# Four products of a state-space scan summed by TensorE instead of being added on VectorE

## What is computed

```python
def s5_mixer(u, lam_re, lam_im, b_re, b_im, c_re, c_im, d, log_dt, w_glu, b_glu):
    ...
    bu = lax.complex(jnp.einsum('blgi,gpi->blgp', uf, jnp.real(b_bar)),
                     jnp.einsum('blgi,gpi->blgp', uf, jnp.imag(b_bar)))
    a = jnp.broadcast_to(lam_bar, bu.shape)
    _, states = lax.associative_scan(diag_combine, (a, bu), axis=1)
    y = (jnp.einsum('blgp,gip->blgi', jnp.real(states), c_re.astype(f32))
         - jnp.einsum('blgp,gip->blgi', jnp.imag(states), c_im.astype(f32))
         + d.astype(f32) * uf)
    y = jax.nn.gelu(y.reshape(B, L, S5_CH))
    y = y * jax.nn.sigmoid(y @ w_glu.astype(f32) + b_glu.astype(f32))
```

## Time and profile before

| | |
|---|---|
| median of three runs | 1843.37 us (1842.34 to 1846.21) |
| the profiled execution | 1846.9 us, its span 1845.1 us |
| TensorE busy | 1667.8 us, 90% of the span |
| VectorE busy | 838.0 us, 45% |
| state-space stretch, layer 0 | 113.2 to 193.9 us |
| state-space stretch, layer 1 | 703.0 to 783.2 us |

### The profile page before, as it was taken

How to read it: one execution, slowest core, us unless ns; L and a number is a source line. 1 busy time by engine, 2 the same in 40 slices (tenths; PEclk the granted TensorE clock), 3 DMA queues, 4 the chain that set the end, 5 groups by cost and what they waited for, 6 DMA issues and landing times.

```text
span 1845.1 us, 23055 instructions
## 1 busy us (share of the span) xinstructions
PE 1667.8 (90%) x9735; PEld 1468.3 (80%) x9735; DVE 838.0 (45%) x1339; ACT 494.1 (27%) x746; POOL 487.9 (26%) x198
## 2 busy tenths in 40 slices
PE   6989889879999898898888999889999988879996
PEld 5877577669999687666667999878888767679996
DVE  3979333324333498923422333338921232154543
ACT  1110330313443111051122444310002221144442
POOL 0000000018887000000003888500000000159883
PEclk9999879899999899987899999999999999889998
DMA  5544223145665453322324666465544312436662
GB/s 131 145 114 110 76 69 103 57 137 162 185 185 168 101 149 103 99 91 64 92 77 130 188 184 187 134 182 143 155 148 133 96 46 64 131 92 184 190 186 70
DMA packets 352775, 233.36 MB, mean 126 GB/s; under 512 B 20070, under 2 KB 339969, under 8 KB 352672
## 3 DMA queue, kind: packets, MB, share of 16 engines
q1 hardware_dynamic: 352672, 231.89, 43.2%
HBM read 230.77 MB, written 1.09 MB: 126 GB/s over the span
## 4 chain that ended last, share of the span: by engine, by line
PE 77%; DVE 13%; ACT 4%; DMA 2%; SPq 2%; issue 1%; POOL 1%; DVEq 0%; ACTq 0%; POOLq 0%
PE ps L1746 20%; PE ps L873 15%; PE ps L1729 6%; PE ps L1731 6%; PE ps L1730 6%; DVE WK L1383 6%; PE ps L856 3%; PE ps L858 3%; PE ps L857 3%; PE ps L895 2%; DVE WK L1541 2%; PE ps L1771 1%; DMA raw<-in_w_in_dram 1%; PE ps L910 1%; PE ps L1798 1%
## 5 line engine op out<-in xcount | busy, mean ns | idle before, releaser
L1111 POOL TENSOR_TENSOR w_lo<-raw,w_hi 128x1024 fp32r<-128x1024 f32 x128 | 320.2, 2503 | 860.7 <-ACT w_hi L1145 857.2
L1746 PE MATMUL ps<-hN,raw 128*128 128x256 f32 (+1 forms) x1376 | 319.3, 394 | 10.0 <-DMA raw<-in_w_in_dram 6.0
L1746 PEld LDWEIGHTS ps<-hN,raw 128*128 128x128 f32 (+1 forms) x1376 | 269.5, 198 | 60.8 <-issue 14.6
L552 POOL TENSOR_TENSOR w_lo<-raw,w_hi 128x1024 fp32r<-128x1024 f32 x66 | 167.5, 2556 | 466.8 <-ACT w_hi L574 466.3
L873 PE MATMUL ps<-hN,raw 128*128 128x256 f32 x896 | 197.7, 383 | 10.3 <-DMA raw<-in_w_in_dram 6.9
L873 PEld LDWEIGHTS ps<-hN,raw 128*128 128x128 f32 x896 | 172.0, 192 | 35.0 <-DMA raw<-in_w_in_dram 7.3
L1145 ACT ACTIVATE w_hi<-raw 128x1024 fp32r<-128x1024 f32 x128 | 135.5, 1059 | 237.8 <-PE ps L1731 144.7
L1729 PE MATMUL ps<-h_hi,w_hi 128*128 128x256 f32 x512 | 145.2, 284 | 10.2 <-DVE h_lo L1383 10.2
L1731 PE MATMUL ps<-c_hi,w_lo 128*128 128x256 f32 x512 | 145.0, 283 | 0.0
L1729 PE MATMUL ps<-c_hi,w_hi 128*128 128x256 f32 x512 | 144.9, 283 | 0.0
L1730 PE MATMUL ps<-c_lo,w_hi 128*128 128x256 f32 x512 | 144.9, 283 | 0.0
(11 more groups left out here) (288 smaller groups left out, 2857.2 us busy)
## 6 DMA issues: line engine op xcount, KB each, us to landing
raw<-in_w_in_dram SPq DMA_DIRECT2D x160, 512.0 KB, 3.8
raw<-in_w_ff_dram SPq DMA_DIRECT2D x128, 512.0 KB, 4.0
raw<-in_w_ffn_in_dram SPq DMA_DIRECT2D x44, 512.0 KB, 3.9
raw<-in_w_ffn_out_dram SPq DMA_DIRECT2D x22, 512.0 KB, 3.3
raw<-in_w_out_dram SPq DMA_DIRECT2D x16, 512.0 KB, 3.6
raw<-in_w_br_s_dram SPq DMA_DIRECT2D x8, 512.0 KB, 3.4
raw<-in_w_br_gla_dram SPq DMA_DIRECT2D x8, 512.0 KB, 3.5
raw<-in_w_br_mla_dram SPq DMA_DIRECT2D x8, 512.0 KB, 3.4
```

What stands on the lines that cost most here:

```text
L552: nc.gpsimd.tensor_tensor(out=w_lo[i % RING][:, 0:kt * n], in0=raw[i % RING][:, 0:kt * n], in1=w_hi[i % RING][:, 0:kt * n], op=ALU.subtrac ...
L1111: nc.gpsimd.tensor_tensor(out=w_lo[i % RING][:, 0:kt * n], in0=raw[i % RING][:, 0:kt * n], in1=w_hi[i % RING][:, 0:kt * n], op=ALU.subtract)\
L1746: last = MM(out, w[:, k, c0:c0 + n], x[:, x0 + k, :], start=k == 0, stop=k == kt - 1)
```

## The change

VectorE no longer adds up the rotation back. It makes the four products alone (one of them negated by a scalar_tensor_tensor), each into a buffer of its own, and TensorE multiplies all four by the same output weights and sums them in PSUM. WA and WD, which only VectorE used in this place before, are now read by TensorE, so the wait for `y_ps` moves from the second write of WC to the start of the group. `y_take` moves from the end of the group to the place before the second scans.

```diff
@@ VectorE, group g
+                    if g:
+                        dve.wait_ge(y_ps.s, y_ps(l, g))
                     tt(WA, B4[:, :, 0, :], c4, ALU.mult)
                     link(tt(WD, B4[:, :, 1, :], s4, ALU.mult))
                     link(tt(WA, WA, WD, ALU.add))
                     scans(WA)
                     tt(WD, B4[:, :, 0, :], s4, ALU.mult)
-                    if g:
-                        dve.wait_ge(y_ps.s, y_ps(l, g))
                     tt(WC, B4[:, :, 1, :], c4, ALU.mult).then_inc(bu_rd.s, 1)
                     dve.wait_ge(bu_rd.s, bu_rd(l, g + 1))
                     link(tt(WC, WC, WD, ALU.subtract))
-                    link(scans(WC))
-
-                    tt(WB, WA, c4, ALU.mult)
-                    link(tt(WD, WC, s4, ALU.mult))
-                    link(tt(WB, WB, WD, ALU.subtract))
-                    tt(WD, WA, s4, ALU.mult)
-                    link(tt(WC, WC, c4, ALU.mult))
-                    tt(WC, WC, WD, ALU.add).then_inc(s_ok.s, 1)
-                    dve.wait_ge(s_ok.s, s_ok(l, g + 1))
-
                     if g:
                         y_take(dve, l, g - 1, stt)
+                    link(scans(WC))
+
+                    tt(WB, WA, c4, ALU.mult)
+                    stt(WD, WC, -1.0, s4, ALU.mult, ALU.mult)
+                    tt(WA, WA, s4, ALU.mult)
+                    tt(WC, WC, c4, ALU.mult).then_inc(s_ok.s, 1)
+                    dve.wait_ge(s_ok.s, s_ok(l, g + 1))
@@ TensorE, y products
-                        MM(PY[cc, 0:T], CT[:, 0, g, cc], W4[1][:, j, :], start=True, stop=False)
-                        last = MM(PY[cc, 0:T], CT[:, 1, g, cc], W4[2][:, j, :], start=False, stop=True)
+                        for n, (r, w) in enumerate(((0, 1), (0, 3), (1, 2), (1, 0))):
+                            last = MM(PY[cc, 0:T], CT[:, r, g, cc], W4[w][:, j, :], start=n == 0, stop=n == 3)
-STEPS_ACT, STEPS_DVE = 7, 275
+STEPS_ACT, STEPS_DVE = 7, 263
```

More of the change, by code:

```diff
@@ L1557, in _ @@
                     link(tt(WC, WC, WD, ALU.subtract))
+                    if g:
+                        y_take(dve, l, g - 1, stt)
                     link(scans(WC))
                     tt(WB, WA, c4, ALU.mult)
-                    link(tt(WD, WC, s4, ALU.mult))
-                    link(tt(WB, WB, WD, ALU.subtract))
-                    tt(WD, WA, s4, ALU.mult)
-                    link(tt(WC, WC, c4, ALU.mult))
-                    tt(WC, WC, WD, ALU.add).then_inc(s_ok.s, 1)
+                    stt(WD, WC, -1.0, s4, ALU.mult, ALU.mult)
+                    tt(WA, WA, s4, ALU.mult)
+                    tt(WC, WC, c4, ALU.mult).then_inc(s_ok.s, 1)
                     dve.wait_ge(s_ok.s, s_ok(l, g + 1))
-                    if g:
-                        y_take(dve, l, g - 1, stt)
                 y_take(dve, l, 3, stt)
```

## The result

The changed kernel took 1852.26 us (median of 5, 1850.51 to 1853.06) against 1842.73 us for the kernel before in the same job: a ratio of 1.0048, 95% interval 1.0033 to 1.0062. The forecast was 1835.2 us, a gain. The profiled execution's span is 1851.3 us against 1845.1.

What follows compares the result with a forecast made beforehand. TensorE bounds most of the kernel, VectorE the y-group stretch of each layer. Savings of 4.4 us (layer 0) and 3.8 (layer 1), 8.2 together, take the median from 1843.37 to 1835.2 us; range 1829 to 1846.

Steps and rivals of the forecast that it cites:

- part (3): TensorE's y products: 16 instead of 8 per group, taking 1.96 us instead of 1.10 at the full clock.
- Rival A: Strips do not all fit TensorE's look-ahead; two at a time, y products take 3.7 us, total 1849; 14%.
- Rival B: Strips' queues run in program order; the 16 y products take 5.8 us, total 1866; 3%.
- The rule of the Trainium skill: On TensorE, matmuls run strictly by program and only weight loads are pulled ahead; by it the change would lose.
- My estimate beside it: TensorE's window of 64 instructions just fits 16 products at two load and two matmul records each, against rival A.
- Part (1): VectorE's group tail: two adds leave, four products in a row take 4.63 us instead of 7.28, saving 2.65 per group.
- Part (2): y_take moved ahead of the second scans: costs VectorE 0.40 us, and y products start 0.05 us behind s_ok everywhere.
- Part (4): New wait: VectorE begins the next group only after the y product, 2.06 us on its chain per group.
- The sum: Both layers' y-group stretches: period 19.19 us, last y product 4.4 us earlier in layer 0, 3.8 in layer 1; 8.2 together.
- The two gaps of TensorE: TensorE's waits in each inner y-group period: 1.3 us before the drive and 0.4 us before the y products.
- The clock: TensorE's clock level follows idle gaps; no drops expected at inner gaps. As a rival, inner drops cost up to 10 us; 9%.
- the last gap: TensorE's wait before a layer's last y product: about 2.8 us, deciding whether query products cost 12.40 or 10.8 us.

Runs made afterwards that it cites:

- e3: Changed kernel without one of the four y products (of WD), three in a row per strip: 1841.56 us, one run.
- e8: Same as e7, but with the y products four in a row for each strip: 1833.31 us, ratio 0.9938 to the kernel before.
- e2: Changed kernel with the y products in two rounds, two in a row for each strip each time: 1838.53 us, one run.
- e10: Same as e1, but with y_take back at the end of the group, behind s_ok: 1841.22 us, one run.
- e5: Kernel before with only the wait for y_ps moved to the start of a group: 1857.39 us, ratio 1.0070.
- e7: Same as e1, plus a second WA and WD for odd groups and the y_ps wait at its old place: 1818.82 us, ratio 0.9857.
- e1: Changed kernel with the y-product loops swapped, one product for each strip in turn: 1833.79 us, ratio 0.9945 to the kernel before.

## Why the prediction was wrong

The sign was wrong. The step that failed is part (3): "each strip runs its own first product, side by side with the others, then its second. So one product of a strip costs 0.43 us, and four take 1.10 + 2 x 0.43 = 1.96 us". The first half is right for two products in a row for each strip. The sum drew on from two to four, which no row of before could carry: with four in a row strips start 0.89 us apart, and the group takes 4.59 us. The term was too small by 2.63 us, eight times, 21 us; the forecast with that term corrected is 1856, and the higher clock behind the stretch gave back part of it. The prediction had named a y group of over 3 us as a sign that it was wrong.

Rival A had the right place, the look-ahead, but priced it at two strips at a time, 3.7 us and 1849. It asked how far back in the program the fourth strip stands. That is not the measure: six back was reached at once, three back in e3 and four back in e8 were not. What counts in these runs is how many products of the *same* strip stand in a row. Rival B, strict order, would have given 5.8 us, and e2's 1.97 us with pairs in a row excludes it, as does the changed kernel's 4.59. The rule of the Trainium skill weighed there (TensorE: Matmul & The Clock Gate, Part 3: Packing small matmuls: matmuls strictly by program) does not describe these traces: in e8's group the second strip's first product starts at 150.91, before the first strip's last at 151.34. By its direction, that the change would lose, it was nearer the truth than my sum, because behind a strip with more than two products in a row the others do wait. My estimate beside it, that the 16 products just fit, spoke against rival A and misled: they took 4.59 us in one order and 1.93 in another.

What held. Part (1): the tail takes 4.63 us and a group 17.12 against 17.13 forecast. Part (2): y_take's 0.40 us (145.56 to 145.96), and its move is worth 0.2 us per group (e10). Part (4): the new wait puts the y group on VectorE's chain, with 0.2 us around it (4.79 against 4.59) where 0.1 was forecast; e5 shows it alone, e7 without it. The sum with its own 1.96 us is e1: 76.55 us in layer 0 against 76.3 forecast. Layer 1 took 78.20, so the stretches gained 6.1 us and not 8.2. That e1's total, 1833.79 us, still lies so near the forecast 1835.2 is partly luck: from the last y product to the GLU products it took 11.42 us in both layers, 6.1 us less than before, which the sum did not count. The two gaps of TensorE came about as forecast in e1. The clock: no drop inside the stretch of the changed kernel. The forecast also had the last gap (2.8, measured 3.30 and 3.31 us) bring the lower level as before; in the changed kernel it did not, which with the logits and query products is the 6.1 us given back. Behind the same gap of 3.3 us the last y group of e1, e2 and e3 fell to the lower level in five of six cases, so this was no sure gain.

What stays open. The rows fit room for two products (four records) of a strip. I have no run with five or more in a row, nor with strips of 64 columns or of rows, so whether the room is counted in products or records, and per strip or per sum in PSUM, isn't settled. Nor is it shown what sets the level behind the last gap, or why e8's profiled span is lower by a further 4.7 us in stages outside the two stretches and their query products.

## What to carry to other kernels

When several small products go to 32-column strips of TensorE, write the loop over the strips innermost; with four products of one strip in a row the same work took 4.59 instead of 1.93 us. Moving additions into PSUM also moves the operands' buffers to TensorE's side: ask which buffers are now read by it and what VectorE can write meanwhile, since two more buffers, with the wait back at its old place, were worth 15 us here (1818.82 against 1833.79). A concurrency that a row shows for n in a row is a price for n in a row, no more.

## What the runs showed of the hardware that I had not expected

- A 32-column strip with more than two float32 products in a row holds up the other strips behind it: 1.97, 2.87 and 4.59 us for two, three and four in a row (16, 12 and 16 products).
- Filling TensorE's waits with useless products made the kernel faster (0.9970, 0.9958 to 0.9983). In layer 0 TensorE then kept its upper level where otherwise the granted clock was 0.80 (before, 194 to 208 us), and from the last y product to the GLU products it took 11.4 instead of 14.2 us; in layer 1 it was 13.1 instead of 14.75, with a drop behind a gap of 1.23 us.
- How long TensorE has stood still does not by itself tell the level that follows: in e5 y groups ran at the upper level behind 3.37 us and at the lower behind 2.77.
